# A tuned two-layer diffusion backbone on one core: the convolution's mean and variance summed by column groups and spread by products with unit columns

## The reference, cut to what matters

```python
def layer_norm(x, g, b):
    xf = x.astype(jnp.float32)
    mu = jnp.mean(xf, axis=-1, keepdims=True)
    var = jnp.mean(jnp.square(xf - mu), axis=-1, keepdims=True)
    y = (xf - mu) * lax.rsqrt(var + EPS)
    return (y * g.astype(jnp.float32) + b.astype(jnp.float32)).astype(x.dtype)

def conv_module(conv_in, w_dw, b_dw, ln_g, ln_b, w_pw2):
    a, b = jnp.split(conv_in, 2, axis=-1)
    u = a * jax.nn.sigmoid(b)
    u = lax.conv_general_dilated(u, w_dw[:, None, :], ...) + b_dw
    u = jax.nn.silu(layer_norm(u, ln_g, ln_b))
    return u @ w_pw2
```

## Time and profile before

| | |
|---|---|
| median of 3 runs | 982.01 us |
| runs | 982.01, 981.21, 996.18 |
| profiled execution | 981.98 us |
| its span on the core | 980.0 us |
| mean granted TensorE clock | 0.985 |
| instructions | 15455 |
| TensorE / VectorE / ScalarE / GpSimd busy | 929.6 / 725.6 / 501.2 / 63.6 us |

### The profile page before, as it was taken

One profiled execution on the slowest core, in us unless ns is written; L12 is line 12 of the kernel. 1 busy time (PEld: TensorE's weight loads), 2 busy tenths in 40 slices (PEclk: granted clock), 3 DMA queues, 4 the chain that ended last, 5 costly groups with the idle time before them and its releaser, 6 DMA issues.

```text
span 980.0 us, 15455 instructions
## 1 busy us (share of the span) xinstructions
PE 929.6 (95%) x5990; PEld 773.4 (79%) x5990; DVE 725.6 (74%) x1210; ACT 501.2 (51%) x716; POOL 63.6 (6%) x62
## 2 busy tenths in 40 slices
PE   3999999989999899999989999998999989999997
PEld 2897788867898778888868968996589977888876
DVE  3568788664855689879956787994658559997895
ACT  4243623285522578647754354226653247774772
POOL 1000000054000000000010000001800000000000
PEclk9999999999999799999999999999999979999999
DMA  9953477601565189949938416652123207994961
GB/s 373 373 206 134 176 291 273 248 1 44 182 248 215 62 320 362 366 156 342 386 120 350 156 64 232 240 214 87 44 88 129 86 28 272 353 383 154 349 264 65
DMA packets 29018, 206.73 MB, mean 211 GB/s; under 512 B 3408, under 2 KB 3440, under 8 KB 4240
## 3 DMA queue, kind: packets, MB, share of 16 engines
q1 hardware_dynamic: 28656, 204.81, 55.5%
q0 software_dynamic: 288, 0.92, 0.3%
HBM read 203.98 MB, written 1.74 MB: 210 GB/s over the span
## 4 chain that ended last, share of the span: by engine, by line
PE 80%; DVE 10%; ACT 4%; issue 3%; DMA 1%; POOL 1%; DVEq 0%; SPq 0%; ACTq 0%
PE ps L860 58%; PE ps L847 6%; PE ps L871 4%; PE ps L1324 2%; PE ps L838 2%; PE ps L1065 1%; PE ps L1148 1%; DVE w_lo L723 1%; ACT w_hi L717 1%; PE ps L1136 1%; DVE x L2325 1%; POOL probs L817 1%; ACT kT L1582 1%; DMA x<-x 1%; DVE w_lo L728 1%
## 5 line engine op out<-in xcount | busy, mean ns | idle before, releaser
L728 DVE TENSOR_TENSOR w_lo<-ring,w_hi 128x2048 fp32r<-128x2048 f32 (+2 forms) x102 | 226.2, 2222 | 28.6 <-ACT w_hi L1688 28.0
L860 PE MATMUL ps<-h_hi,w_hi 128*128 128x384 f32 x576 | 198.7, 345 | 6.3 <-issue 2.4
L1688 ACT ACTIVATE w_hi<-ring 128x2048 fp32r<-128x2048 f32 x96 | 183.3, 1914 | 30.3 <-PE ps L860 30.3
L860 PE MATMUL ps<-h_hi,w_lo 128*128 128x384 f32 x576 | 193.6, 336 | 0.0
L860 PE MATMUL ps<-h_lo,w_hi 128*128 128x384 f32 x576 | 193.5, 336 | 0.0
L860 PEld LDWEIGHTS ps<-h_hi,w_hi 128*128 128x128 f32 x576 | 108.1, 188 | 22.5 <-issue 14.6
L723 DVE TENSOR_TENSOR w_lo<-ring,w_hi 128x2048 fp32r<-128x2048 f32 x41 | 93.7, 2289 | 39.8 <-ACT w_hi L717 39.8
L860 PEld LDWEIGHTS ps<-h_lo,w_hi 128*128 128x128 f32 x576 | 108.2, 188 | 0.0
L860 PEld LDWEIGHTS ps<-h_hi,w_lo 128*128 128x128 f32 x576 | 108.1, 188 | 0.0
L1932 DVE SCALAR_TENSOR_TENSOR z<-u,par,z 128x399 f32<-128x399 f32 x180 | 104.7, 630 | 1.5
L860 PE MATMUL ps<-w_hi,hg_hi 128*128 128x512 f32 x256 | 103.6, 405 | 1.1 <-DVE w_lo L728 1.0
(11 more groups left out here) (269 smaller groups left out, 1434.5 us busy)
## 6 DMA issues: line engine op xcount, KB each, us to landing
ring<-wpre SPq DMA_DIRECT2D x96, 1024.0 KB, 6.8
ring<-wmoe SPq DMA_DIRECT2D x96, 1024.0 KB, 6.1
x<-x SPq DMA_DIRECT2D x1, 1536.0 KB, 7.7
x_out<-x SPq DMA_DIRECT2D x4, 384.0 KB, 2.3
par<-par_in POOLq DMA_DIRECT2D x2, 367.5 KB, 4.8
const<-const_in SPq DMA_DIRECT2D x1, 314.0 KB, 3.0
ckv_out<-ckvT POOLq DMA_DIRECT2D x2, 64.0 KB, 5.2
kr_out<-kr POOLq DMA_DIRECT2D x2, 16.0 KB, 5.8
```

The source lines that it names most:

```text
L728: return nc.vector.tensor_tensor(out, whole, leading.bitcast(F32), ALU.subtract)
L860: m = mm(out, a, b, start=(start and i == 0 and j == 0), stop=(stop and i == n - 1 and j == 2))
L1688: af(w_hi[m % MOE_PLACES], slot(moe_slot(l, m)), ACT.Copy).then_inc(split_hi, 1)
```

## The change

Four edits, the same in both layers.

1. The mean and the variance are each summed by `quarter_sums`: 4 chunks x 4 column groups, 100 columns (ZQ) each, into 32 rows each. As 4 x 100 is one more than 399, the last group takes columns 299 to 398. The sum now stands as 128x100.
2. ScalarE copies the mean's quarters from PSUM to `rs` (a new instruction ahead of its qT copies), and TensorE spreads them to 128x399 in a new job "mspread", placed between qT 1 and qT 2. VectorE subtracts out of that job's bank.
3. The Sqrt and the reciprocal work on 128x100 instead of 128x399. TensorE spreads the reciprocal in a new job "vspread", placed between kT 2 and kT 3; it waits there on a new semaphore, `dev_rooted`. VectorE multiplies `z` by it out of PSUM.
4. Two jobs more in the list, so that the banks of qT, var and kT change: the first score's bank 0 was last used by kT 7 and is now last used by kT 5. A wait ahead of the Silu is added.

```diff
--- before.py
+++ after.py
@@ -71,6 +71,8 @@
 ADA_BANK = 7
 
 QTOK = TOK // 4
+
+ZQ = 100
 
 COND_AT = 32 - 2
 
@@ -292,12 +294,16 @@
     for c in range(KD):
         add("gate", 2 * c, "act")
         add("gate", 2 * c + 1, "act")
-    add("mean", 0, "dve")
+    add("mean", 0, "act")
     for h in range(H):
         add("qT", h, "act")
+        if h == 1:
+            add("mspread", 0, "dve")
     add("var", 0, "act")
     for h in range(H):
         add("kT", h, "act")
+        if h == 2:
+            add("vspread", 0, "dve")
     for kind, n in attention_steps():
         if kind == "scores":
             add("s", n, "act", SCORE_BANKS[n % 3])
@@ -614,6 +620,7 @@
         taps_spread = sem("taps_spread")
         pool_order = sem("pool_order")
         z_squared = sem("z_squared")
+        dev_rooted = sem("dev_rooted")
         z_normed = sem("z_normed")
         conv_act = sem("conv_act")
         max_ready = sem("max_ready")
@@ -1096,10 +1103,30 @@
                     for e in adas_after(l, "gate", c):
                         ada(e)
 
+                def quarter_sums(out, chunk):
+
+                    for c in range(KC):
+                        for j in range(QUADS):
+                            a = min(j * ZQ, Z_W - ZQ)
+                            b = a + ZQ
+                            m = mm(out[QUAD * j:QUAD * (j + 1), 0:ZQ], ones[:, 0:QUAD], chunk(c, a, b),
+                                   start=(c == 0), stop=(c == KC - 1))
+                            if c + j == 0:
+                                first(m)
+                    m.then_inc(psum_full, 1)
+
+                def spread_quarters(name):
+                    out = begin(name)
+                    for j in range(QUADS):
+                        a, b = j * ZQ, min((j + 1) * ZQ, Z_W)
+                        row = ident[:, QUAD * j:QUAD * j + 1].broadcast_to([P, P])
+                        m = mm(out[:, a:b], row, rs[:, ZQ - (b - a):ZQ], start=(j == 0), stop=(j == QUADS - 1))
+                    m.then_inc(psum_full, 1)
+
                 out = begin("mean")
                 pe.wait_ge(conv_done, l + 1)
                 wait_taken(pe, l, "csum")
-                product(out[:, 0:Z_W], [ones] * KC, [z[:, c, :] for c in range(KC)]).then_inc(psum_full, 1)
+                quarter_sums(out, lambda c, a, b: z[:, c, a:b])
 
 
                 for n, (name, tiles) in enumerate((("qT", TT), ("kT", KT))):
@@ -1109,12 +1136,17 @@
                         out = begin(name, hd)
                         transposes(out[0:QK, :], [q[:, t, hd, :] if n == 0 else k[:, t, hd, :] for t in range(tiles)]
                                    ).then_inc(psum_full, 1)
+                        if n == 0 and hd == 1:
+                            wait_taken(pe, l, "mean")
+                            spread_quarters("mspread")
+                        if n == 1 and hd == 2:
+                            pe.wait_ge(dev_rooted, l + 1)
+                            spread_quarters("vspread")
                     if n == 0:
                         out = begin("var")
 
                         pe.wait_ge(z_squared, l + 1)
-                        product(out[:, 0:Z_W], [ones] * KC, [u[:, c, HALF:HALF + Z_W] for c in range(KC)]
-                                ).then_inc(psum_full, 1)
+                        quarter_sums(out, lambda c, a, b: u[:, c, HALF + a:HALF + b])
                         ada_columns(batches_before(l, "ada") + 1)
 
                 def scores(i):
@@ -1568,15 +1600,17 @@
                     af(gates[:, c, :], ps_of("gate", c)[:, 0:TOK], ACT.Sigmoid).then_inc(taken["act"], 1)
                     if c % 2 and 8 + c // 2 < EARLY_SPLITS:
                         hi(8 + c // 2)
+                wait_full(act, l, "mean")
+                af(rs[:, 0:ZQ], ps_of("mean")[:, 0:ZQ], ACT.Copy).then_inc(taken["act"], 1)
                 for hd in range(H):
                     wait_full(act, l, "qT", hd)
                     af(qT[0:QK, hd, :], ps_of("qT", hd)[0:QK, 0:TOK], ACT.Copy).then_inc(taken["act"], 1)
                     if hd == 3:
 
-                        wait_taken(act, l, "mean")
+                        wait_taken(act, l, "mspread")
                         af(u[:, :, HALF:HALF + Z_W], z[:, :, :], ACT.Square).then_inc(z_squared, 1)
                 wait_full(act, l, "var")
-                af(rs[:, :], ps_of("var")[:, 0:Z_W], ACT.Sqrt, bias=eps[:, 0:1], scale=1.0 / DC).then_inc(taken["act"], 1)
+                af(rs[:, 0:ZQ], ps_of("var")[:, 0:ZQ], ACT.Sqrt, bias=eps[:, 0:1], scale=1.0 / DC).then_inc(taken["act"], 1)
                 for hd in range(H):
                     wait_full(act, l, "kT", hd)
                     af(kT[0:QK, hd, :], ps_of("kT", hd)[0:QK, :], ACT.Copy).then_inc(taken["act"], 1)
@@ -1617,6 +1651,7 @@
                 hi(EARLY_SPLITS + 2)
 
                 act.wait_ge(z_normed, l + 1)
+                wait_taken(act, l, "vspread")
                 for c in range(KC):
                     m = af(z[:, c, :], z[:, c, :], ACT.Silu, scale=pf("ln_g")[:, c:c + 1], bias=pf("ln_b")[:, c:c + 1])
                 chain(m)
@@ -2035,16 +2070,19 @@
                 ada_copy(batches_before(l, "ada") + 1)
                 assert sum(taps_done) == KC * TAPS
 
-                wait_full(dve, l, "mean")
+                wait_full(dve, l, "mspread")
                 for c in range(KC):
-                    m = stt(z[:, c, :], ps_of("mean")[:, 0:Z_W], -1.0 / DC, z[:, c, :], ALU.mult, ALU.add)
+                    m = stt(z[:, c, :], ps_of("mspread")[:, 0:Z_W], -1.0 / DC, z[:, c, :], ALU.mult, ALU.add)
                 m.then_inc(taken["dve"], 1)
                 wait_taken(dve, l, "var")
-                chain(nc.vector.reciprocal(rs[:, :], rs[:, :]))
-                wait_taken(dve, l, "mean")
+                nc.vector.reciprocal(rs[:, 0:ZQ], rs[:, 0:ZQ]).then_inc(dev_rooted, 1)
+                wait_taken(dve, l, "mspread")
+                wait_full(dve, l, "vspread")
                 for c in range(KC):
-                    m = vt(z[:, c, :], z[:, c, :], rs[:, :], ALU.mult)
-                m.then_inc(z_normed, 1)
+                    m = vt(z[:, c, :], z[:, c, :], ps_of("vspread")[:, 0:Z_W], ALU.mult)
+                    if c == KC - 2:
+                        m.then_inc(z_normed, 1)
+                m.then_inc(taken["dve"], 1)
                 ada_finish(batches_before(l, "ada") + 1, mod[:, 2 * ADA_FIRST:2 * ADA_UNITS, :],
                            pf("b_ada")[:, 0:2 * (ADA_UNITS - ADA_FIRST)], ADA_UNITS - ADA_FIRST)
                 dve.wait_ge(adaT_taken, batches_before(l, "ada") + 1)
```

## The result

| | before | changed |
|---|---|---|
| median, first comparison | 989.1 us (981.21 to 997.01, 4 runs) | 996.23 us (995.37 to 997.5, 4 runs) |
| ratio, from the executions of before near 981 alone | 1 | 1.015, 95% interval 1.0126 to 1.0174 |
| profiled execution | 981.98, span 980.0 | 996.19, span 994.4 |
| mean granted TensorE clock | 0.985 | 0.965 |

Against the kernel before's executions near 981 the changed kernel is 1.5% slower, 14 us; that is less than two per cent, but outside the range of 980.0 to 985.0 that I gave. Between the medians it is 7.1 us. The times can't be read without one fact: the kernel before itself has executions near 981 and near 996 (the 996.18 among the three runs at the top was one), and the interval compares the changed kernel only with the former.

What follows compares the result with a forecast made beforehand. The prediction took the chain of waits around the convolution's LayerNorm, up to the attention's first Exp, as what prices the change. +0.27 us a layer, +0.54 over two, on 981.98 gave 982.5 us; range 980.0 to 985.0.

Steps and rivals of the forecast that it cites:

- whatever moves the first Exp moves all behind it: LayerNorm of layer 0 to attention: any shift of the attention's first Exp (204.59) passes to everything after it.
- the runs of before alone differ by 0.8: Argument for the range: the kernel before's own runs were given as 981.21 and 982.01 us.
- The rival of a falling clock: TensorE idling in the LayerNorm drops to half clock at 197: about 4 us a layer, 990 us; chance 0.07.
- The price of 4: Half rate during spread, five kT heads and first attention: up to 1.0 + 2.2 + 2 us, about 4 a layer.
- The local sum: Main case, LayerNorm to first Exp: kT 3 late, +0.27 us a layer, 982.5 us in all; chance 0.74.
- Mean: Layer 0: quarter sums, copy and spread start VectorE's subtraction at 191.55 instead of 191.77, a gain of 0.22 us.
- Variance: Layer 0: Sqrt starts at 197.94 against 198.46, and the kT copies can begin 1.0 us earlier than 199.28.
- Spread: Variance's spread ahead of kT 3 waits for the reciprocal; ScalarE idles 1.2 us; kT copies end at 203.55, before 203.28.
- the term a layer: Net change of the LayerNorm stretch per layer: +0.27 us, bounds +0.1 and +0.45.
- the prediction's own mark: The mean's start, from which the first Exp was to come 0.1 to 0.45 us later.
- the root's gain lost in the wait of kT 3: kT copies begin 1.0 us earlier, but kT 3 stands behind the variance's spread and ScalarE idles 1.2 us.
- 62 ns a matmul: Skill's sequencer price, 2.0 us instead of 0.67 for 32 quarter products; set aside because 48 loads took 0.98 us.

Runs made afterwards that it cites:

- e2: The kernel before, unaltered, timed again under a second name: median 985.4 us (981.25 to 998.25).
- e6: The kernel before with one extra, unused Square of 128x1024 on ScalarE in layer 0: median 984.8 us, all twelve between 983.5 and 986.9.
- e9: Only the mean's half of the change, on the kernel before with the gather in pairs: median 977.9 us.
- e10: Only the variance's half of the change, on the kernel before with the gather in pairs: median 980.2 us.
- e3: The changed kernel with the variance's spread moved on TensorE from behind kT 2 to behind kT 5: median 988.2 us.
- the gather in pairs: The kernel before with the gather's 32-row shift products in fours instead of twos, so 24 dense products run in one piece: median 978.5 us.

## Why the prediction was wrong

**The step that failed** is "whatever moves the first Exp moves all behind it". I took the program behind the attention as rigid, and so priced the change by a stretch of 16 us alone. The rows of the low clock at 323 were in my hands, but I read them as evidence on whether the clock would fall in the LayerNorm, and did not ask what ends that stretch. Nor did I ask why one of the three runs of the kernel before stood at 996.18, which was the size of the effect: 15 us; "the runs of before alone differ by 0.8" leaves that run out. The kernel before, unaltered, has a median of 985.4 in e2, so the range of 980.0 to 985.0 would have been a matter of luck without any change. Both questions could have been put to the profile of before; that the answer for this change would be "late" could not be had from it, as e6 shows, where a shift did good.

**The rival of a falling clock** was right in kind and wrong in place and price. It did fall in the LayerNorm of layer 0, from 194.69 to 198.11, near where I had put it (197). From the mean's first load to the first Exp layer 0 took 203.30 - 187.16 = 16.14 us, layer 1, without a fall, 689.38 - 673.54 = 15.84: about 0.3 us, not 4. The price of 4 rested on a low clock during the spread, five kT heads and the head of the attention, and the clock was back as the spread began (198.00). The loss was 130 us further on.

**The local sum**, term by term (layer 1 of the changed kernel):
- Mean. I had the subtraction 2.70 us after the adaLN unit (191.55 against 188.85); it started after 2.39 (676.32). From first load to copy I had 0.94 us and it took 1.15 (673.54 to 674.69); but the load came 0.39 us ahead of the unit's end and not 0.07, so that the copy began 0.76 behind the unit where I had 0.87. The copy took 0.25, as estimated. The spread's first load came 1.21 behind the unit (675.14) where I had 1.45: behind the quarter products TensorE's loads stood idle for 0.15 us, not up to 0.3. From there to VectorE it was 1.18, not 1.24.
- Variance. From Square to the end of the table load 4.33, as taken (4.34); the Sqrt followed with no wait; the reciprocal took 0.78, as taken.
- Spread. Load to VectorE 1.24 (683.92 to 685.16), as taken. TensorE's reaction was 0.05, not 0.12, and from load to the kT copy it was 1.61, not 1.83. So the gap on ScalarE was 1.02, not 1.2.
- Together 0.31 + 0.07 + 0.22 = 0.60, less 0.04 in the other terms, makes the 0.56 by which the Exp came earlier than in my sum (15.45 against 16.01). The sign of the term a layer turned from +0.27 to -0.29: the mean's half gave 0.54 (e9) where I had 0.22, and the variance's half cost 0.25 (e10) where I had 0.49. By the first load, the prediction's own mark, the term is +0.03, and the first Exp hardly moved. That was small beside the 14 us, and the mechanism (the root's gain lost in the wait of kT 3) held, as e3 and e10 show.

**62 ns a matmul.** The price that the Trainium skill, page "TensorE: Matmul & The Clock Gate", section "Wait — 56ns, not 53.3ns?", gives for matmuls decoded by microcode did not bind here, as I had taken it: the 32 quarter products took 0.87 and 0.89 us, 27 to 28 ns each.

## What to carry to other kernels

Before pricing a local edit, list the stretches in which TensorE's clock is low, and ask of each what ends it; if one kernel's runs differ by more than its edits could make, that is the first thing to explain. Where such a stretch crosses a rhythm of dense and thin products, a shift in time ahead of it can cost or save more than the edit itself, as it did here, so price an edit in a form of the kernel that doesn't have this sensitivity. A product put between two operations of another engine must be placed by when its input is ready: behind kT 5 the same spread cost nothing, behind kT 2 it cost 1.1 us.

## What the runs showed of the hardware

- A TensorE busy without a break can stay at the half clock: in the changed kernel's gather from 329 to 344 us, 12 products of 128 rows and two of 32 in turn, all at half rate. With 24 dense products in a run no stretch was longer than 13.7 us in the profiled executions.
- One program had low stretches of 10.24 and 27.32 us behind the router in different executions, and a Square of 1 us added ahead of it left no execution above 986.9 in twelve.
- In 14 stretches with this gather the length went with the distance from the clock's fall to the gather's first product: short at 6.03 to 7.33 us, long at 5.02 or less and at 7.43 or more. With the gather in pairs 4.46 us gave a short one and 7.44 one of 13.65.
- Behind other column-group work, 32 quarter products of 128x100 took 0.87 us (673.75 to 674.62) and added 0.69 to the chain, as the first begin before the previous ones have ended (673.93).
- Not settled: why the length goes with this distance, and why all nine executions of the changed kernel are of the long kind, while the kernel before has both.
